# An encoder layer with sixteen experts: the final norm of ten row tiles regrouped, and identity transposes around the first gather

## The reference, cut to what matters

```python
x = x + mixers(x)                                   # not touched by the change
h = rmsnorm(x, norm_ffn)
aff = softmax(h @ w_router)                         # T = 1280 tokens, 16 experts
gates, idx = top_k(aff.T, cap)                      # 128 of 1024 prompt tokens, 32 of 256 sample tokens
for e in range(16):
    xe = h[idx[e]]
    ye = (silu(xe @ w_gate[e]) * (xe @ w_up[e])) @ w_down[e]      # 1024 -> 2816 -> 1024
    x[idx[e]] += gates[e] * ye
return rmsnorm(x, norm_final)                       # the final norm
```

## Time and profile before

| | |
|---|---|
| median of three runs | 2585.72 us (2581.74 to 2586.13) |
| profiled execution | 2586.17 us, its span 2584.3 us |
| mean granted TensorE clock | 0.974 |
| TensorE matmuls busy | 2449.8 us, 95% |
| VectorE, ScalarE, POOL busy | 1638.5, 1346.8, 155.9 us |
| DMA | 628.13 MB, mean 243 GB/s |

### The profile page before, as it was taken

How to read it: one execution, slowest core, us unless ns; L and a number is a source line. 1 busy time by engine, 2 the same in 40 slices (tenths; PEclk the granted TensorE clock), 3 DMA queues, 4 the chain that set the end, 5 groups by cost and what they waited for, 6 DMA issues and landing times.

```text
span 2584.3 us, 44975 instructions
## 1 busy us (share of the span) xinstructions
PE 2449.8 (95%) x18271; PEld 1917.9 (74%) x18271; DVE 1638.5 (63%) x1367; ACT 1346.8 (52%) x1243; POOL 155.9 (6%) x207
## 2 busy tenths in 40 slices
PE   6999999299999999999999999999999999999997
PEld 5888788277777777777777777777777777777775
DVE  4433448766666666767576757675767576757575
ACT  5322223255555565656565656565656565655565
POOL 0021000000100000000001000000010101000101
PEclk8999999599999999999999999999999999999998
DMA  5102142447878787878777877778787868686877
GB/s 188 33 17 74 52 162 106 157 174 278 307 276 286 274 287 274 298 269 303 269 293 269 297 274 284 277 281 290 268 293 266 304 254 307 252 319 240 321 271 279
DMA packets 295967, 628.13 MB, mean 243 GB/s; under 512 B 21360, under 2 KB 72688, under 8 KB 295536
## 3 DMA queue, kind: packets, MB, share of 16 engines
q1 hardware_dynamic: 284160, 587.87, 62.1%
q0 software_dynamic: 11632, 37.51, 4.9%
HBM read 599.10 MB, written 26.21 MB: 242 GB/s over the span
## 4 chain that ended last, share of the span: by engine, by line
PE 90%; DVE 4%; issue 3%; ACT 2%; DMA 1%; POOL 0%; SPq 0%; POOLq 0%; DVEq 0%; ACTq 0%
PE ps L378 21%; PE ps L379 20%; PE ps L380 20%; PE ps L1508 12%; PE ps L1297 8%; PE ps L1516 6%; PE ps L1526 1%; DVE i L1050 1%; DVE v L1048 1%; DVE A L1052 1%; ACT win_h L626 1%; PE ps L1467 1%; DVE win_l L891 1%; DMA raw<-in_w_down_dram 0%; PE ps L1535 0%
## 5 line engine op out<-in xcount | busy, mean ns | idle before, releaser
L1180 DVE TENSOR_TENSOR spl_l<-raw,spl_h 128x2048 fp32r<-128x2048 f32 x528 | 1208.6, 2292 | 577.7 <-ACT spl_h L782 560.5
L782 ACT ACTIVATE spl_h<-raw 128x2048 fp32r<-128x2048 f32 x528 | 1011.8, 1917 | 569.9 <-PE ps L380 520.0
L379 PE MATMUL ps<-spl_l,xT 128*128 128x512 f32 x1408 | 556.6, 395 | 31.5 <-issue 31.5
L378 PE MATMUL ps<-spl_h,xT 128*128 128x512 f32 x1408 | 560.7, 398 | 6.0 <-issue 3.5
L380 PE MATMUL ps<-spl_h,xT 128*128 128x512 f32 x1408 | 554.1, 394 | 0.0
L379 PEld LDWEIGHTS ps<-spl_l,xT 128*128 128x128 f32 x1408 | 268.2, 190 | 91.1 <-issue 37.0
L378 PEld LDWEIGHTS ps<-spl_h,xT 128*128 128x128 f32 x1408 | 267.8, 190 | 82.8 <-issue 26.2
L1508 PE MATMUL ps<-raw,xTs 128*32 128x256 f32 (+1 forms) x6144 | 314.2, 362 | 0.0
L380 PEld LDWEIGHTS ps<-spl_h,xT 128*128 128x128 f32 x1408 | 268.1, 190 | 57.1
L378 PE MATMUL ps<-spl_h,g 128*128 128x512 f32 x704 | 278.3, 395 | 2.4 <-DVE spl_l L1180 2.4
L379 PE MATMUL ps<-spl_l,g 128*128 128x512 f32 x704 | 274.5, 390 | 0.0
(11 more groups left out here) (229 smaller groups left out, 1904.6 us busy)
## 6 DMA issues: line engine op xcount, KB each, us to landing
raw<-in_w_up_dram SPq DMA_DIRECT2D x352, 512.0 KB, 7.8
raw<-in_w_gate_dram SPq DMA_DIRECT2D x352, 512.0 KB, 8.7
raw<-in_w_down_dram SPq DMA_DIRECT2D x176, 1024.0 KB, 13.9
win_raw<-in_w_in_dram SPq DMA_DIRECT2D x16, 512.0 KB, 3.9
xt<-in_x_dram SPq DMA_DIRECT2D x10, 512.0 KB, 8.8
xr<-in_x_dram SPq DMA_DIRECT2D x10, 512.0 KB, 4.1
acc_dram<-xr SPq DMA_DIRECT2D x10, 512.0 KB, 2.6
xn_dram<-xn SPq DMA_DIRECT2D x10, 512.0 KB, 2.8
```

The costliest lines, as they stand in the source:

```text
L378: eng.matmul(o, a_h, b_h, start=first, stop=False, skip_group_check=True)
L379: eng.matmul(o, a_h, b_l, start=False, stop=False, skip_group_check=True)
L782: act.activation(spl_h[:, i % SPL, :], raw[:, slot_of(i), :], ACT.Copy).then_inc(sh_ok, 1)
L1180: dve.tensor_tensor(spl_l[:, i % SPL, :], raw[:, slot_of(i), :], spl_h[:, i % SPL, :].bitcast(F32), ALU.subtract).then_inc(sl_ok, 1)
```

## The change

The final norm moves into the sample blocks b = 1, 2 and 3 of the last expert: tiles 0 to 2, 3 to 5 and 6 to 9. In a block ScalarE does all squares first (`row_squares`) and then all roots (`row_root`), between its gs copy and the Silu; VectorE does all scalings before the sample's product. The first six squares write their unused output to `fj`, which lies over `accP` in SBUF, so the gathers into `accP` and `accS` move behind the sixth square. `HOME` gives each tile its buffer; a load into a used buffer waits for the store before it. On TensorE 48 transposes of the identity matrix, whose result nobody reads, stand ahead of the first gather's transposes, and 24 behind them.

```diff
-NORMS = {INS + 2: (0,), INS + 3: (1,), INS + 4: (2,), INS + 5: (3,), INS + 6: (4,), INS + 8: (5,), INS + 9: (6, 7),
-         INS + 10: (8, 9)}
+NORMS = {1: (0, 1, 2), 2: (3, 4, 5), 3: (6, 7, 8, 9)}
+HOME = (0, 1, 2, 0, 1, 2, 3, 4, 0, 1)
...
+        fj = at("fj", 99 * KB, [P, D])
...
@@ POOL
             def load_rows(t):
-                pool.dma_start(fx[t % FX][:, :], acc_t[t]).then_inc(f_in[t % FX], 16)
+                s = HOME[t]
+                if HOME[:t].count(s):
+                    pool.wait_ge(f_out[s], 16 * HOME[:t].count(s))
+                pool.dma_start(fx[s][:, :], acc_t[t]).then_inc(f_in[s], 16)
...
+            pool.wait_ge(xg_ps, E)
+            for t in range(3):
+                load_rows(t)
+            for t in range(3):
+                store_rows(t)
+            for t in range(3, 6):
+                load_rows(t)
+            pool.wait_ge(fs_ok, 6)
             pool.wait_ge(cg_ok, E * 4)
             pool.indirect_dma_start(accP[:, :], None, acc,
                                     bass.IndirectOffsetOnAxis(sidx[:, 0:1], 0)).then_inc(acc_in, 16)
             pool.indirect_dma_start(accS[:, :], None, acc_q,
                                     bass.IndirectOffsetOnAxis(sidx[:, 1:2], 0)).then_inc(acc_in, 16)
-            pool.wait_ge(xg_ps, E)
-            for t in range(3):
+            pool.wait_ge(pe_unit, (E - 1) * UNITS + INS)
+            for t in range(6, 8):
                 load_rows(t)
-            pool.wait_ge(pe_s, (E - 1) * SAMPLE + NC)
-            for t in range(3, FX):
+            for t in range(3, 6):
+                store_rows(t)
+            for t in range(8, TILES):
                 load_rows(t)
-            for t in range(2):
-                store_rows(t)
-            for t in range(2, TILES):
-                if t + 3 < TILES:
-                    pool.wait_ge(f_out[(t + 3) % FX], 16)
-                    load_rows(t + 3)
+            for t in range(6, TILES):
                 store_rows(t)
@@ ACT
-            def row_norm(t):
-                if t == 0:
+            def row_squares(t):
+                s = HOME[t]
+                act.wait_ge(f_in[s], 16 * (HOME[:t].count(s) + 1))
+                if t:
+                    act.wait_ge(fs_ok, t)
+                if t == 6:
                     act.wait_ge(p_ok, E * NC)
-                act.wait_ge(f_in[t % FX], 16 * (t // FX + 1))
-                act.activation(bank(4, 2), fx[t % FX][:, :], ACT.Square, accum_out=fss[:, t:t + 1]).then_inc(fs_ok, 1)
+                act.activation(fj[:, :] if t < 6 else bank(4, 2), fx[s][:, :], ACT.Square, accum_out=fss[:, t:t + 1]).then_inc(fs_ok, 1)
+
+            def row_root(t):
                 act.wait_ge(fs_ok, t + 1)
                 act.activation(fss[:, TILES + t:TILES + t + 1], fss[:, t:t + 1], ACT.Sqrt, bias=eps[:, 0:1],
                                scale=1.0 / D).then_inc(frt_ok, 1)
...
                             product_s(e, b - 1)
+                        if last:
+                            for t in NORMS.get(b, ()):
+                                row_squares(t)
+                            for t in NORMS.get(b, ()):
+                                row_root(t)
                         if b < NB:
                             silu_s(e, b)
...
-                    if last:
-                        for t in NORMS.get(i, ()):
-                            row_norm(t)
@@ DVE
                                 product_lo(e, c)
+                        if last:
+                            for t in NORMS.get(b, ()):
+                                row_scale(t)
                         if b < NB:
                             product_s(e, b)
...
-                        for t in NORMS.get(i, ()):
-                            row_scale(t)
@@ PE
+            def idle_turns(count):
+                for _ in range(count):
+                    pe.transpose(bank(0)[:, 0:P], ident[:, :], ident[:, :])
...
+            idle_turns(48)
             gathered(1)
+            idle_turns(24)
             expert(0, False)
```

More of the change, by code:

```diff
@@ L482, in _ @@
             for s in range(FX):
-                sp.wait_ge(f_out[s], 16 * len(range(s, TILES, FX)))
+                sp.wait_ge(f_out[s], 16 * HOME.count(s))
             sp.wait_ge(z_out, 32)
@@ L564, in load_rows @@
             def load_rows(t):
-                pool.dma_start(fx[t % FX][:, :], acc_t[t]).then_inc(f_in[t % FX], 16)
+                s = HOME[t]
+                if HOME[:t].count(s):
+                    pool.wait_ge(f_out[s], 16 * HOME[:t].count(s))
+                pool.dma_start(fx[s][:, :], acc_t[t]).then_inc(f_in[s], 16)
             def store_rows(t):
                 pool.wait_ge(fo_ok, t + 1)
-                pool.dma_start(out_t[t], fx[t % FX][:, :]).then_inc(f_out[t % FX], 16)
+                pool.dma_start(out_t[t], fx[HOME[t]][:, :]).then_inc(f_out[HOME[t]], 16)
             pool.wait_ge(added[0], (E - 1) * 16)
@@ L585, in _ @@
                                     bass.IndirectOffsetOnAxis(sidx[:, 1:2], 0)).then_inc(acc_in, 16)
-            pool.wait_ge(xg_ps, E)
-            for t in range(3):
+            pool.wait_ge(pe_unit, (E - 1) * UNITS + INS)
+            for t in range(6, 8):
                 load_rows(t)
-            pool.wait_ge(pe_s, (E - 1) * SAMPLE + NC)
-            for t in range(3, FX):
+            for t in range(3, 6):
+                store_rows(t)
+            for t in range(8, TILES):
                 load_rows(t)
-            for t in range(2):
-                store_rows(t)
-            for t in range(2, TILES):
-                if t + 3 < TILES:
-                    pool.wait_ge(f_out[(t + 3) % FX], 16)
-                    load_rows(t + 3)
+            for t in range(6, TILES):
                 store_rows(t)
             for s in range(FX):
-                pool.wait_ge(f_out[s], 16 * len(range(s, TILES, FX)))
+                pool.wait_ge(f_out[s], 16 * HOME.count(s))
             pool.wait_ge(z_ok, 1)
@@ L1215, in row_scale @@
                 dve.wait_ge(fr_ok, t + 1)
-                dve.scalar_tensor_tensor(out=fx[t % FX][:, :], in0=fx[t % FX][:, :], scalar=frr[:, t:t + 1], in1=gfin[:, :],
+                s = HOME[t]
+                dve.scalar_tensor_tensor(out=fx[s][:, :], in0=fx[s][:, :], scalar=frr[:, t:t + 1], in1=gfin[:, :],
                                          op0=ALU.mult, op1=ALU.mult).then_inc(fo_ok, 1)
@@ L1245, in expert @@
                             gathered_lo(e + 2)
-                    if last:
-                        if i == 0:
-                            adder()
-                        for t in NORMS.get(i, ()):
-                            row_scale(t)
+                    if last and i == 0:
+                        adder()
             dve.memset(pvs[:, 0, :], 0.0).then_inc(pS_ok, 1)
```

## The result

| | before | after |
|---|---|---|
| median | 2585.93 us (2581.74 to 2587.72, 4 runs) | 2547.63 us (2544.52 to 2548.36, 4 runs) |
| span of the profiled execution | 2584.3 us | 2542.7 us |
| mean granted TensorE clock | 0.974 | 0.985 |

The ratio is 0.9852, 95% interval 0.9835 to 0.9869. The forecast was 2596.7 us, range 2580 to 2602.

A forecast was written before the change was run, and what follows sets the result against it. The prediction took TensorE, 90% of the chain, as the bound, with the tail hanging on the tenth row tile. Its terms, -6.6 + 7.3 + 0.8 + 1.9 + 7.2 + 1.6 - 1.2 = +11.0, gave 2596.7 us, range 2580 to 2602.

The forecast's parts named there:

- part 6: Around the first gather: 72 added transposes raise TensorE's clock for the first matmuls; -1.2 us, bounds 0 and -2.6.
- The term for the loop: Loop over experts 1 to 14: code untouched by the diff, so no change forecast, 0 us.
- the rivals: Last expert: row tiles move unnoticed beside weights, 2577.5 us, chance 0.15; only part collides, 2582.9 us, chance 0.20.
- Part 1: Kernel's end: earlier scaling of tiles 6 to 9 lets the accP sum directly follow the last unit; -6.6 us.
- Part 3: Last expert, block 1: row-tile stores and loads delay weights of units 19 to 21; +7.3 us, plus 0.8 for clock.
- part 4: Last expert, block 2: row-tile transfers and gathers delay down weights; 4.3 less the earlier 2.4, so +1.9 us.
- Part 2: Last expert, blocks 1 and 2: the groups' ScalarE and VectorE time fits into idle room; costs nothing.
- Part 5: Last expert, group 3: late down weights and norm work delay unit 32's split; +7.2 us, plus 1.6 for clock.
- a wait of up to 4 us remains, which can drop the clock again: Before the first gather's transposes: TensorE may still wait after the 48 turns and lose its raised clock.

The follow-up runs named there:

- e1: Kernel before with the 48 and 24 transposes alone, final norm as before: 2535.66 us, ratio 0.9806.
- e3: Kernel before with all 72 transposes early, ahead of the list transposes, none around the first gather: 2535.43 us, ratio 0.9808.
- e7: Number not defined in the text given; seemingly a run with TensorE's loop head placed at another instruction slot; its time can't be assigned.
- e11: Number not defined in the text given; seemingly another run with TensorE's loop head placed at a chosen slot; its time can't be assigned.
- e6: Kernel after, with stores of tiles 0 to 2 and loads of 3 to 5 held until TensorE has done 19 last-expert units: 2538.1 us, ratio 0.9817.
- e2: Kernel after without any of the 72 transposes, so the regrouped norm alone: 2599.75 us, ratio 1.0051 to the kernel before.
- slot 230: Kernel before with TensorE's expert loop starting at instruction slot 230 of its block of 256: 2582.67 us, ratio 0.9985.
- slot 64: Kernel before with TensorE's expert loop starting at instruction slot 64 of its block of 256: 2590.22 us, ratio 1.0018.
- e12: Kernel before with the loop head at slot 160 and tiles normed one by one, two or three units earlier, the tenth by one: 2530.24 us, ratio 0.9791.
- slot 200: Kernel before with TensorE's expert loop starting at instruction slot 200 of its block of 256: 2542.09 us, ratio 0.9838.
- slot 160: Kernel before with TensorE's expert loop starting at instruction slot 160 of its block of 256: 2535.19 us, ratio 0.9805.

## Why the prediction was wrong

**The step that failed** is in part 6: "72 turns" were costed by what they do (warm the clock, bounds 0 and -2.6), and "No other engine waits for them" closed the account. The loop behind them was taken as unchanged because its code is. The term for the loop was nothing, without a reason given; measured, it is -50.5. Their 144 instructions moved the head from about slot 232 to about 120, and that is worth 50 us, shown by e1, e3, e7 and e11. The page's chain had "issue 3%", some 78 us, and the earlier trace rows showed a stop of 3.48 us by "issue", which I used only as a price for the clock. The 13 others stand in a row of the page of the kernel before, ahead of any experiment (busy, mean ns, idle and what ended it):

```profile
L379 PE MATMUL ps<-spl_l,xT 128*128 128x512 f32 x1408 | 556.6, 395 | 31.5 <-issue 31.5
```

I had read the waits view from 2400 us on only. None of the rivals had this.

**Part 1, right.** Forecast -6.6: the sum directly behind the last unit, 14.1 us ahead of the end. VectorE, kernel after:

```profile
2520.87 2.28 DVE L1195 TENSOR_TENSOR spl_l<-raw,spl_h 128x2048 fp32r<-128x2048 f32 x1
2528.74 1.28 DVE L1288 SCALAR_TENSOR_TENSOR accP<-ps,cgate,accP 128x1024 f32<-128x1024 f32 x1 [5.58 <-PE ps L381]
```

VectorE waits for TensorE at 2528.74, and 14.0 us remain to the end of the span.

**Parts 2 to 4.** The waits of the earlier trace rows have become these; ScalarE, then TensorE, kernel after:

```profile
2447.95 1.92 ACT L790 ACTIVATE spl_h<-raw 128x2048 fp32r<-128x2048 f32 x1 [2.09 <-DMA raw<-in_w_gate_dram]
2453.02 1.92 ACT L790 ACTIVATE spl_h<-raw 128x2048 fp32r<-128x2048 f32 x1 [2.67 <-DMA raw<-in_w_gate_dram]
2460.05 1.91 ACT L790 ACTIVATE spl_h<-raw 128x2048 fp32r<-128x2048 f32 x1 [5.11 <-DMA raw<-in_w_gate_dram]
...
2497.51 1.91 ACT L790 ACTIVATE spl_h<-raw 128x2048 fp32r<-128x2048 f32 x1 [3.06 <-DMA raw<-in_w_down_dram]
2502.37 1.91 ACT L790 ACTIVATE spl_h<-raw 128x2048 fp32r<-128x2048 f32 x1 [2.95 <-DMA raw<-in_w_down_dram]
2506.22 1.91 ACT L790 ACTIVATE spl_h<-raw 128x2048 fp32r<-128x2048 f32 x1 [1.94 <-DMA raw<-in_w_down_dram]
```

```profile
2452.24 0.50 PE L379 MATMUL ps<-spl_h,xT 128*128 128x512 f32 x1 [0.25 <-DVE spl_l L1195]
2457.32 0.50 PE L379 MATMUL ps<-spl_h,xT 128*128 128x512 f32 x1 [2.06 <-DVE spl_l L1195]
2464.34 0.79 PE L379 MATMUL ps<-spl_h,xT 128*128 128x512 f32 x1 [3.98 <-DVE spl_l L1195]
...
2523.21 0.80 PE L379 MATMUL ps<-spl_h,g 128*128 128x512 f32 x1 [6.54 <-DVE spl_l L1195]
```

Part 3 forecast three stops, 7.3 us, plus 0.8 of clock: they are 0.3, 2.1 and 4.0, together 6.3, and behind the last seven matmuls run at the lower clock (0.79, then 0.43 apart), 1.6 us. e6 shows that the transfers caused them: with the three stores and the three loads held back they are gone, and ScalarE's and VectorE's work of group 1 is still there. Stores and loads were not held back one without the other. Of parts 4 and 5 in block 2 the same waits view that had 2.4 in the earlier trace rows has 15.9 us in six for the last expert; less 6.3 and unit 32's 6.5, that leaves 3.1 ahead of unit 32, against the 4.3 that part 4 worked out before it took off the 2.4 of before. Part 2 holds in block 1: TensorE's first wait there is at 2452.24, behind a split for which ScalarE waited 2.09 us for a gate weight, and so not behind the group's own work.

**Part 5, right.** Forecast 7.2 us ahead of unit 32 with splits that wait for down weights; measured 6.54, with ScalarE's three waits of 3.06, 2.95 and 1.94 before it. The chain that ended last runs as part 5 has it: the weight of unit 31 (2506.20), four squares from 2508.89, the table, the scalings from 2515.49, the split of unit 32 at 2520.87. All twelve matmuls of unit 32 then run 0.43 apart, 2.4 us lost against 1.6 forecast.

Parts 1 to 5 summed to +12.2; the last expert took 13.0 more, and e2, which has only these parts, is 2599.75 us, 14.4 above the kernel before in the same runs. With part 6 at nothing the forecast for e2 would have been 2597.9. That the sums agree so well is in part luck: by the rows above the parts are -6.6, 7.9, 0.7 and 8.9, together 10.9, and e1's last expert, without any group, is 3.0 us longer than the one before.

**Part 6, the front.** Forecast -1.2 between 0 and -2.6. TensorE, kernel after, to be set beside the earlier trace rows:

```profile
501.85 0.30 PE L1476 MATMUL ps<-ident,qidxf 48*128 48x48 f32 x1
502.08 8.35 PE L1481 MATMUL ps<-ident 128*128 128x128 f32 x48
513.31 1.06 PE L1487 MATMUL ps<-ident,xg 128*128 128x128 f32 x8 [2.88 <-DMA xgs<-xn_dram,qidxT]
514.21 0.38 PE L1489 MATMUL ps<-ident,xgs 128*128 128x128 f32 x2
514.43 2.78 PE L1481 MATMUL ps<-ident 128*128 128x128 f32 x24
517.14 0.47 PE L379 MATMUL ps<-spl_h,xT 128*128 128x512 f32 x1
```

The eight transposes take 1.06 us instead of 1.94, and the first matmuls are 0.23 apart from the first on. The step "a wait of up to 4 us remains, which can drop the clock again" did not come true here at 2.88 us, so the whole bound of 2.6 was had in this stretch of the profile. It did in e1, at 3.04: the granted clock was 0.50 from 515 to 518, the 24 transposes took 4.45 us instead of 2.78 and held the first matmul up, and only 1.0 of the 2.6 was had. The other 1.5 of the 4.1 were there already at the lists' transposes (501.85 against 503.36), ahead of every transpose added; the profiles of kernels without transposes ahead of that point differ by up to 3.6 us there (501.10 with slot 230, 504.73 with slot 64).

## What to carry to other kernels

Before costing a change, read the chain's "issue" share and the waits view of the whole kernel, above all for an engine's own issue waits whose count is near that of the loop's passes: an edit ahead of a loop moves the loop in the instruction stream, and with it these stops. Where they occur, place the loop before tuning anything else, and compare versions of other parts only with the loop at the same place: here a change worth +12 to +14 us looked like -38. In block 1, 3.15 MB added beside a weight stream with 0.4 us of slack were paid for in full (7.9 us at 0.4 MB per us, 7.9 us of stops and lower clock), while moving the tiles a little earlier one by one (e12) gained 5 us where the groups lost 12.

## What the runs showed that was not expected

- The place of a loop of 2058 instructions within 256 slots is worth 50 us of 2586 in 14 passes: 2.2 to 2.6 us (slots 230 and 232) or up to 3.3 us (slot 64) of stop per pass, and 0.3 or 1.9 us more behind it (periods of 127.1 and 128.7 us before, 124.4 without a stop).
- Behind a branch, or behind the loop's end, TensorE went on past the next boundary 5.0 to 5.1 us after its first matmul, whether six, seven, ten or eleven matmuls came before the stop; with 22 (5.0 us) there was next to none.
- After stops of 2.44 us the matmuls came 0.43 apart in some passes and not in others: between 772 and 782 us the granted clock was 0.83, between 1030 and 1040, around another pass's stop, 1.00. After waits of 3.98, 5.00 and 6.54 us the first matmul took 0.79 to 0.80 us.
- Why the stop at the branch ends between slots 64 and 96, and why TensorE waits for the low part in slot 200's loop and not in slot 160's, stays open.
